# A reordered attention stretch and three other reordered stretches in a two-block fp32 kernel on one core

## What is computed

```python
# first block, layer 0: gated linear recurrence ("hgrn"), layer 1: differential attention
h = h + rms_norm(mixer(rms_norm(h, pre)), post)
h = h + rms_norm(squared_relu_mlp(rms_norm(h, mlp_pre)), mlp_post)
k, v = rms_norm(h, kv_norm) @ w_kv                     # after layer 0, used by layer 1
p = softmax(q @ k.T * scale + rel_bias, block-causal)  # two maps for each of 8 heads
o = (p[0] - lam * p[1]) @ v;  o = rms_norm(o, subln) * c;  mix = o @ w_out
# second block
z = rmsnorm(x, mix_pre) @ w_in                         # cq, ckv, k_rope, b, c, x parts
a = mla(...);  c = short_gated_conv(b, c, x)
x = x + rmsnorm(concat(rmsnorm(a), rmsnorm(c)) @ w_out, mix_post)
x = x + rmsnorm((silu(h @ w_gate) * (h @ w_up)) @ w_down, ffn_post)
x = x + sigmoid(x @ w_ple_gate) * rmsnorm(p @ w_ple_proj, ple_norm)
```

## Time and profile before

| | us |
| --- | --- |
| median of 3 runs | 1073.61 |
| lowest, highest | 1071.01, 1073.74 |
| the profiled execution | 1073.17 |
| its span on the core | 1071.4 |
| busy in it: TensorE matmul (PE) | 1017.5 |
| busy in it: VectorE (DVE) | 734.1 |
| busy in it: ScalarE (ACT) | 550.2 |

### The profile page before, as it was taken

How to read it: one execution, slowest core, us unless ns; L and a number is a source line. 1 busy time by engine, 2 the same in 40 slices (tenths; PEclk the granted TensorE clock), 3 DMA queues, 4 the chain that set the end, 5 groups by cost and what they waited for, 6 DMA issues and landing times.

```text
span 1071.4 us, 18148 instructions
## 1 busy us (share of the span) xinstructions
PE 1017.5 (95%) x6659; PEld 921.8 (86%) x6659; DVE 734.1 (69%) x1097; ACT 550.2 (51%) x822; POOL 91.7 (9%) x95
## 2 busy tenths in 40 slices
PE   6999999999999999777999999998998999999997
PEld 5999988888888998776788888997997788888886
DVE  4687677877745577644787754467857887776466
ACT  4743255655454465443565544344556565556444
POOL 5123101000101100000100010101000100000010
PEclk9999999999999999998999999999999999999999
DMA  8443334556565744322366665624533366665641
GB/s 248 132 137 119 119 118 138 166 188 195 177 196 180 234 148 148 98 80 73 117 214 194 186 189 185 189 67 126 177 99 103 114 192 194 183 195 172 192 148 60
DMA packets 163758, 165.74 MB, mean 155 GB/s; under 512 B 6736, under 2 KB 161504, under 8 KB 163696
## 3 DMA queue, kind: packets, MB, share of 16 engines
q1 hardware_dynamic: 162496, 163.47, 49.8%
q0 software_dynamic: 1056, 1.16, 0.5%
q10 hardware_dynamic: 144, 0.26, 0.1%
HBM read 163.79 MB, written 1.08 MB: 154 GB/s over the span
## 4 chain that ended last, share of the span: by engine, by line
PE 86%; DVE 8%; issue 3%; ACT 3%; DMA 0%; POOL 0%; DVEq 0%; ACTq 0%; POOLq 0%
PE ps L591 30%; PE ps L590 15%; PE ps L574 4%; PE ps L575 4%; PE ps L576 4%; PE ps L587 3%; PE ps L811 3%; PE ps L570 2%; PE ps L569 2%; PE ps L568 2%; DVE w_lo L1790 2%; PE ps L708 2%; PE ps L588 2%; PE ps L581 1%; PE ps L583 1%
## 5 line engine op out<-in xcount | busy, mean ns | idle before, releaser
L1790 DVE TENSOR_TENSOR w_lo<-w_raw,w_hi 128x1024 fp32r<-128x1024 f32 (+3 forms) x318 | 381.0, 1203 | 188.0 <-ACT w_hi L1279 183.0
L1279 ACT ACTIVATE w_hi<-w_raw 128x1024 fp32r<-128x1024 f32 x302 | 317.4, 1054 | 231.4 <-PE ps L591 91.4
L591 PE MATMUL ps<-xs,w_hi 128*128 128x512 f32 x840 | 296.9, 396 | 0.0
L590 PE MATMUL ps<-xs,w_lo 128*128 128x256 f32 x840 | 235.7, 281 | 0.0
L591 PEld LDWEIGHTS ps<-xs,w_hi 128*128 128x128 f32 x840 | 157.8, 188 | 34.5
L591 PE MATMUL ps<-us,w_hi 128*128 128x512 f32 x498 | 175.1, 397 | 0.0
L590 PEld LDWEIGHTS ps<-xs,w_lo 128*128 128x128 f32 x840 | 158.2, 188 | 5.2 <-DVE xs L1923 1.7
L590 PE MATMUL ps<-us,w_lo 128*128 128x256 f32 x498 | 139.2, 280 | 0.0
L574 PE MATMUL ps<-xs,w_hi 128*128 128x256 f32 x384 | 113.5, 296 | 5.7 <-DVE w_lo L1790 4.5
L591 PEld LDWEIGHTS ps<-us,w_hi 128*128 128x128 f32 x498 | 93.5, 188 | 22.3
L575 PE MATMUL ps<-xs,w_hi 128*128 128x256 f32 x384 | 110.1, 287 | 0.0
(11 more groups left out here) (375 smaller groups left out, 1709.4 us busy)
## 6 DMA issues: line engine op xcount, KB each, us to landing
w_raw<-in_mlp_w_up SPq DMA_DIRECT2D x64, 512.0 KB, 4.4
w_raw<-in_mlp_w_down SPq DMA_DIRECT2D x64, 512.0 KB, 3.5
w_raw<-in_a_w_in SPq DMA_DIRECT2D x32, 512.0 KB, 3.9
w_raw<-in_w_gate SPq DMA_DIRECT2D x22, 512.0 KB, 3.7
w_raw<-in_w_up SPq DMA_DIRECT2D x22, 512.0 KB, 4.6
w_raw<-in_w_down SPq DMA_DIRECT2D x20, 512.0 KB, 4.3
w_raw<-in_w_kv SPq DMA_DIRECT2D x16, 512.0 KB, 4.4
w_raw<-in_w_in SPq DMA_DIRECT2D x16, 512.0 KB, 3.9
```

Of the source, the lines that this page charges most:

```text
L590: mm(ps[:, bank, 0:S], lo[:, kk, w], x[:, kt, 0:S], start=False, stop=False)
L591: o = mm(ps[:, bank, :], hi[:, kk, w], x[:, kt, :], start=False, stop=last)
L1279: o = fn(dst, raw, ACT.Copy)
L1790: return v.tensor_tensor(d, x, y, ALU.subtract)
```

## The change

In attention the units are taken in the order ak0, ak1, ak2, aq0, aq1, aq2, ak3, aq3, av0 to av3 (before, av0 stood third). `hi` and `lo` of a step are those of q + 3 where they were of q + 4. `scores(g)` runs at q = 8 + g without a break, `turn(g)` at q = 10 + g (it was 11 + g, then 12 + g), `copy_turned(g)` at 11 + g; `values` at 18, 20, 22 and after the loop (it was 14, 20, 22 and after). The pair steps move with them. Signs are turned so that a minimum replaces the maximum and one small multiply in `add_bias` goes.

In the head the identity and the first norm's weights are loaded ahead of the other tables; both engines make the halves of x straight from the transposes' PSUM banks, and the copy to `h` comes behind them. One activation table is loaded at the start. In mix, `hi` and `lo` of c0 and uq go ahead of the norm of mix_pre, `hi` of c0 goes behind `narrow_high("cq")`, and `sums("cq")` behind both quanta of c0. In out2, ScalarE's squares of the attention output and VectorE's `take2(5)` go behind the halves of the convolution, and the copies of `ple` are taken in another order. In the tail the last pair of `pg` is computed in token order, one token tile after the other; h and ple of its features are transposed ahead of it, the other rows in between and behind, and five output DMAs replace four.

```diff
           ("a_out", 1, 4), ("up0", 1, 16), ("down0", 4, 4),
-          ("ak0", 0, 0), ("ak1", 0, 0), ("av0", 0, 0), ("aq0", 0, 0), ("aq1", 0, 0), ("ak2", 0, 0), ("aq2", 0, 0), ("ak3", 0, 0),
-          ("aq3", 0, 0), ("av1", 0, 0), ("av2", 0, 0), ("av3", 0, 0), ("b_out", 1, 4), ("up1", 1, 16), ("down1", 4, 4),
+          ("ak0", 0, 0), ("ak1", 0, 0), ("ak2", 0, 0), ("aq0", 0, 0), ("aq1", 0, 0), ("aq2", 0, 0), ("ak3", 0, 0), ("aq3", 0, 0),
+          ("av0", 0, 0), ("av1", 0, 0), ("av2", 0, 0), ("av3", 0, 0), ("b_out", 1, 4), ("up1", 1, 16), ("down1", 4, 4),
           ("cq", 0, 0), ("ckv", 0, 0), ("kr", 0, 0), ("c0", 0, 0), ("uq", 0, 0), ("x0", 0, 0), ("ukv", 0, 0),
           ("b0", 0, 0), ("c1", 0, 0), ("x1", 0, 0), ("b1", 0, 0), ("ple", 0, 0), ("out2", 1, 4), ("gu", 1, 22),
...
+            for m in range(2):
+                sp.wait_ge(row_copied[0], m + 1)
+                sp.dma_start(out[0, m * P:(m + 1) * P, 0:512], rowbuf[:, m, 0:512]).then_inc(out_done, 16)
+            sp.wait_ge(row_copied[2], 1)
+            sp.dma_start(out[0, 0:P, 768:D], rowbuf[:, 0, 768:D]).then_inc(out_done, 16)
+            sp.wait_ge(row_copied[1], 1)
+            sp.dma_start(out[0].rearrange("(m p) n -> p m n", p=P)[:, :, 512:768], rowbuf[:, :, 512:768]).then_inc(out_done, 16)
+            sp.wait_ge(row_copied[2], 2)
+            sp.dma_start(out[0, P:S, 768:D], rowbuf[:, 1, 768:D]).then_inc(out_done, 16)
+            sp.wait_ge(out_done, 80)
 
...
-                                split_unit(u, 8 * j, last_kt, x, kind, pset)
+                                split_unit(u, 8 * j, last_kt, x, kind, pset, between_tiles)
...
 
-            pe.wait_ge(tab_in, 16)
+            pe.wait_ge(ident_in, 16)
+            pe.wait_ge(pre_in, 16)
+            nc.tensor.transpose(ps[:, 3, 0:KT], vrow_pre[:, :], ident[0:KT, 0:KT]).then_inc(pre_turned, 1)
             xrow = mo[:, :, :].rearrange("p a b -> p (a b)").rearrange("p (m n) -> p m n", m=2)
...
+                elif j == 2:
                     pe.wait_ge(xs_ready, XS0["attn"] + 1)
-                elif j > 1:
-                    pe.wait_ge(max_ready, N_GROUPS)
                 for hh in range(2):
                     hd = 2 * j + hh
...
                     pe.wait_ge(hankel_masked, 1)
-                if 8 <= q <= 16:
+                if 8 <= q < 8 + N_GROUPS:
                     scores(q - 8)
-                elif 18 <= q <= 20:
-                    scores(q - 9)
-                if 11 <= q <= 19:
-                    turn(q - 11)
-                elif q >= 21:
-                    turn(q - 12)
-                if q in (14, 20, 22):
-                    values((14, 20, 22).index(q))
-                if q in (17, 22):
-                    turn_pair((17, 22).index(q))
-
-            def second_pair():
+                if 10 <= q < 10 + N_GROUPS:
+                    turn(q - 10)
+                if q in (18, 20, 22):
+                    values(q // 2 - 9)
+                if q in (21, 22):
+                    turn_pair(q - 21)
+
+            def last_pairs():
+                values(3)
                 turn_pair(2)
-                values(3)
 
             stream("b_out", xs_b, waits=xs_wait("attn"), two=True,
-                   between={1: second_pair, 5: lambda: turn_pair(3)})
+                   between={1: last_pairs, 5: lambda: turn_pair(3)})
             sums("b_post")
             keep_streaming(9)
...
             narrow("c0", 0).then_inc(w_used, 1)
+            narrow("c0", 1).then_inc(w_used, 1)
             sums("cq")
-            narrow("c0", 1).then_inc(w_used, 1)
 
             def short_tile(name, kt, cols, bank, n, xi, first, last):
...
+            def turn_last():
+                pe.wait_ge(xs_ready, XS0["last"] + KT)
+                for n, (src, bank) in enumerate(((h, B5), (ple, B7))):
+                    for m in range(2):
+                        for t in range(2):
+                            o = nc.tensor.transpose(ps[:, bank, m * S + t * P:m * S + (t + 1) * P],
+                                                    src[:, 6 + t, m * P:(m + 1) * P], ident)
+                    o.then_inc(last_turned, 1)
+
+            def turn_rows():
+                pe.wait_ge(pg_mul, 2)
                 for m in range(2):
...
+                        o = nc.tensor.transpose(ps[:, 4 + 2 * m, t * P:(t + 1) * P], h[:, t, m * P:(m + 1) * P], ident)
                     o.then_inc(row_turned, 1)
...
+            stream("pg", xs, waits=xs_wait("last"), two=True, after=turn_last, between_tiles=turn_rows)
+            pe.wait_ge(pg_mul, 3)
+            pe.wait_ge(last_taken, 1)
+            for m in range(2):
+                for t in range(2):
+                    o = nc.tensor.transpose(ps[:, B5, m * S + t * P:m * S + (t + 1) * P], h[:, 4 + t, m * P:(m + 1) * P], ident)
+            o.then_inc(row_turned, 1)
...
 
-            act.dma_start(table[:, 0:T_LEVEL], a["tables"][:, 0:T_LEVEL]).then_inc(tab_in, 16)
+            act.dma_start(table[:, 0:P], a["tables"][:, 0:P]).then_inc(ident_in, 16)
...
 
+            root_tables()
             act.wait_ge(pre_ready, 1)
             for j in range(4):
-                high_w(xs, V_A_PRE, None, [j])
+                act.wait_ge(x_turned, j + 1)
+                for t in range(2):
+                    o = fn(xs[:, 2 * j + t, 0:S], ps[:, 4 + j, t * S:(t + 1) * S], ACT.Copy,
+                           scale=vec[:, V_A_PRE + 2 * j + t:V_A_PRE + 2 * j + t + 1])
+                o.then_inc(xs_hi, 1)
                 hi(j // 2, part=j % 2)
...
-            hi_d(7)
             high_w(xs_b, V_B_PRE, 1, (2, 3))
             root("kv_b")
             for q in range(4, 24):
-                hi_d(q + 4)
-                if q == 6:
-                    take_v(0)
-                if q in (20, 22):
+                hi_d(q + 3)
+                if q in (22, 23):
+                    high_pair(q - 22)
+                if q in (18, 20, 22):
                     take_v(q // 2 - 9)
-                if 12 <= q <= 20:
-                    copy_turned(q - 12)
-                elif q >= 22:
-                    copy_turned(q - 13)
-                if 9 <= q <= 17:
+                if 11 <= q < 11 + N_GROUPS:
+                    copy_turned(q - 11)
+                if 9 <= q < 9 + N_GROUPS:
                     exps(q - 9)
-                elif 19 <= q <= 21:
-                    exps(q - 10)
-                if q in (15, 21, 23):
-                    square_pair((15, 21, 23).index(q))
-                if q in (16, 22):
-                    root_pair((16, 22).index(q))
-                if q in (18, 23):
-                    high_pair((18, 23).index(q))
+                if q in (19, 21, 23):
+                    square_pair((q - 19) // 2)
+                if q in (20, 21, 23):
+                    root_pair((20, 21, 23).index(q))
+            hi_d(27)
             take_v(3)
-            copy_turned(11)
-            root_pair(2)
             high_pair(2)
...
             hi(UNIT0["kr"], part=1)
+            narrow_high("cq", V_Q, 0)
             hi(UNIT0["c0"], part=0)
-            narrow_high("cq", V_Q, 0)
-            root("mix_pre")
             hi(UNIT0["c0"], part=1)
-            narrow_high("ckv", V_KV2, 2)
             for part in range(2):
                 hi(UNIT0["uq"], part=part)
+            root("mix_pre")
+            narrow_high("ckv", V_KV2, 2)
             root_eps("cq")
             hi(UNIT0["x0"], part=0)
...
-            square_tok(1)
             high("conv", 0, cy, xs_m)
             high("conv", 1, cy, xs_m)
+            square_tok(1)
+
+            def take_ple(j):
+                fn(ple[:, 2 * j:2 * j + 2, :], ps[:, PLE_BANK[j], :].rearrange("p (a t) -> p a t", a=2), ACT.Copy)\
+                    .then_inc(z_act, 1)
+
+            act.wait_ge(w_used, 2 * (UNIT0["ple"] + 1))
+            take_ple(2)
+            hi(UNIT0["out2"] + 1, part=0)
             act.wait_ge(att_ms, 1)
...
+            take_ple(0)
+            take_ple(1)
+            hi(UNIT0["out2"] + 1, part=1)
+            take_ple(3)
...
+            for j in range(3):
+                one("pg", j)
+                act.wait_ge(pg_sum, j + 1)
+                fn(mo[:, 2 * j:2 * j + 2, :], mo[:, 2 * j:2 * j + 2, :], ACT.Sigmoid).then_inc(pg_sig, 1)
+                if j == 0:
+                    act.wait_ge(last_turned, 1)
+                    fn(rowbuf[:, :, 768:D], ps[:, B5, :].rearrange("p (m c) -> p m c", m=2), ACT.Copy).then_inc(last_taken, 1)
+            act.wait_ge(tail_done, len(POSTS) + 1)
+            fn(mo[:, 6, :], ps[:, LAST_BANK, 0:S], ACT.Sigmoid).then_inc(pg_sig, 1)
             for m in range(2):
                 act.wait_ge(row_turned, m + 1)
                 fn(rowbuf[:, m, 0:512], ps[:, 4 + 2 * m, :], ACT.Copy).then_inc(row_copied[0], 1)
+            act.wait_ge(w_used, 2 * N_UNITS)
+            fn(mo[:, 7, :], ps[:, LAST_BANK + 1, 0:S], ACT.Sigmoid).then_inc(pg_sig, 1)
+            act.wait_ge(row_turned, 3)
```

(67 more changed lines are left out.)

96 lines of the change are left out of this document (29 added, 67 removed).

## The result

The changed kernel takes 1044.42 us (median of four runs, 1044.17 to 1045.1) where the kernel before took 1072.31 (1070.67 to 1073.74): 27.9 us less, a ratio of 0.974 with a 95% interval of 0.972 to 0.976. Its profiled execution took 1044.17 us, with a span of 1042.4 against 1071.4.

What follows compares the result with a forecast made beforehand. TensorE, its matmuls busy 95% of the span, was taken as the bound, so only its stalls and slow clock count. 19.5 + 2.0 + 1.5 + 1.9 + 0.8 = 25.7 us; 1073.17 - 25.7 = 1047.5 us, range 1044.5 to 1053.5.

Steps and rivals of the forecast that it cites:

- The stall of attention: Attention: transposes' waits at L928 (12.0 us), behind ScalarE's copy, go; whole attention sum 19.5 us, 19.9 by counting work left.
- The pair chains at the end of attention: End of attention: pair 2's turn no longer waits (L952, 2.4 us); pair 3's is due at 16.1, ready at 14.4.
- third rival: End of attention: transposes' waits go, the pair chain's remain, 8 to 10 us stay: 1057 us; chance 0.05.
- The lead of one quantum less: Attention: conversions lose one quantum of lead; low halves of q + 3 end at T + 4.6, needed three 3.9 us steps later.
- second rival: Attention: VectorE's full steps become the period, 0.5 us over for twelve steps, 6 us: 1053.5 us; chance 0.12.
- fourth rival: Attention: combine(g) too late for turn(g) in its step; a whole quantum late costs 31 us: 1078.5 us; chance 0.03.
- Kept, 2.4 at L587: After attention: the 2.4 us wait at L587, which the change doesn't touch, stays.
- Head: Start of kernel: third low half at 14.5 us, second matmul run 2.2 us sooner; 2.0 us taken, ends 1.0 and 3.0.
- Mix: Mix stage: TensorE's 4.23 us wait becomes waits of 1.2, 1.6 and 0.9; 1.5 us gained, ends 0 and 2.4.
- first rival: Mix: the gaps it gets in exchange (3.7 us within 9 us) lower the clock, some 1.6 us: 1049.1 us; chance 0.10.
- Out2: Out2: second start goes from 812.30 to 810.4; 1.9 us gained, ends 0.8 and 2.3.
- tail: End of kernel: last row ready at 1068.1, before 1068.87; 0.8 us gained, ends -0.5 and 1.6.

Runs made afterwards that it cites:

- the new plan with the stall left in it: Changed kernel with attention's conversions back at their old lead (hi_d(q + 4), lo_d(q + 4)), still ahead of copy_turned: 1069.99 us.
- the last one: Changed kernel with four edits: GpSimd's copy held, c0 and cq's sums reordered in mix, pair 0 of b_out sooner, tail copies later: 1037.38 us.

## Why the prediction was right, and where not

The forecast was 25.7 us, made against the profiled execution, where it was 29.0 (27.9 between the medians). The steps in their order:

- **The stall of attention**: right. The copy behind a conversion causes it (moving the copy alone removes all 12.0 us), the new lead and order end it, and TensorE's step is the forecast 3.9 us. The sum, 19.5, measured 20.3, near the 19.9 of the second way of counting, which I had not taken.
- **The pair chains at the end of attention**: right that they no longer wait. How much hangs on them was not in the text: the third rival put 8 to 10 us on them, and the copy moved alone shows 5.7 us of waits plus clock come back there. The two halves of the change need each other: order alone gives 6 us, the new plan with the stall left in it costs some 4, both together give 20.3.
- **The lead of one quantum less**: the text counted its cost (nothing, low halves are early enough) and missed its use. It lets the exponentials follow their scores without a conversion that waits in between, 9 us by the run with the old lead behind the copy.
- **VectorE as the next bound (second rival)**: it didn't come. The margin is 0.7 to 0.8 us a step, wider than the 0.3 that "3.6 of 3.9" says, because full and light steps alternate and one lends to the other. The fourth rival's place is right (the transposes wait for `combine`), its price too high: a late `combine` costs its own lateness, not a quantum.
- **"Kept, 2.4 at L587" with no clock change**: the profile shows 1.3 us gained there. It is no effect of the change: the kernel before with only the copy moved has 17.62 us there. Thirteen kernels ran that stretch, and without the last one, which shortens the wait, four of them took 17.6 to 17.7 us and eight 19.0 to 19.2. The kernel before (18.99) and the changed one (17.67) fell on different sides.
- **Head**: the step 14.5 was 14.72, right, though not by the walk as written: ScalarE began at 6.64 us and not 7.1, and the first conversion waited for its weights until 8.52, which the text had landing at 7.6. The gain was 2.6 us at the stage behind it (137.64 to 135.01), where 2.0 was taken and the text had 0.6 to add if the clock rises 3.4 us sooner. It rose 3.3 us sooner in this execution. The run with later transposes, with the same head, was 1.67 us better still, all of it clock; so this term's upper end should have been 4.3, not 3.0.
- **Mix**: 2.1 us for 1.5, within its ends, and the three waits of 1.46, 1.47 and 0.84 stand where 1.2, 1.6 and 0.9 were forecast. One step was wrong in kind: "the rotation costs nothing". It starts GpSimd's copy, and that holds VectorE's critical chain for 1.6 us. It did so before as well, beside uq's low halves, which is why the sum came out right: a cost of the same size was moved, and I had seen it in neither place. The first rival (a lower clock in mix) didn't come: the granted clock is 1.00 from 700 to 760 us.
- **Out2** 1.85 for 1.9, with waits of 0.47 and 0.45 where "some 0.5" was said; **tail** 0.6 for 0.8, with 0.99 of wait for 1.05.

The time came out at the low end of the stated range, 0.1 us past it (1044.42 for 1044.5). Two terms of clock, some 0.6 us in the head and 1.3 behind `b_out`, fell on the good side together; the first had been given too short an upper end and the second none. The second is luck of the execution, as the traces of kernels that are the same in that stretch differ by as much. The first is less so: the gain of 2.6 us lies between the 1.6 and 4.4 that the other profiled kernels with this head show against the kernel before, so the term was rather set too low. The rest of the 3.3 us between forecast and trace is 0.8 in attention and 0.6 in mix, and smaller pieces that cancel.

## What to carry to other kernels

An in-order queue is read from its waits: where an instruction that waits for the bottleneck engine stands in front of one that frees a buffer for it, swap them first, and then look at once for the chain that the stall had hidden, because one of the two edits alone may give a quarter of what both give. When an engine that is nearly full sets the pace, compare each of its operations with the same operation elsewhere in the trace; one that takes five times as long may be held up by another engine, which no view of waits will show; move the other engine's operation and look again. And price a margin by the engine's own waits over several steps, not by its fullest step.
